# The first eight units of a two-block transformer kernel: the first unit split chunk by chunk, six units laid out in 8 KB runs, rotation tables loaded apart, and banks of their own for units 2 and 3 (counted from 0)

## What is computed

```python
normed = rms_norm(h, mix_norm_pre[0])
proj = normed @ w_in                       # 1024 x 6144
q, k, v, g = jnp.split(proj, [h * dk, 2 * h * dk, 2 * h * dk + h * dv], axis=-1)
q = rotate_pairs(q, cos, sin)
k = rotate_pairs(k, cos, sin) * (dk ** -0.5)
...                                        # decayed scores, o = scores @ v, norm, silu(g) * o, @ w_out
...                                        # FFN; block with sparse attention; FFN
...                                        # second block: gMLP and window attention, then 16 experts
```

## Time and profile before

| | us |
|---|---|
| median of 3 runs (2026.28 to 2027.13) | 2027.04 |
| the profiled execution's own time | 2029.09 |
| its span (first to last instruction) | 2027.3 |
| PE busy in the span | 1610.7 |
| DVE busy | 753.9 |
| ACT busy | 559.8 |

### The profile page before, as it was taken

How to read it: one execution, slowest core, us unless ns; L and a number is a source line. 1 busy time by engine, 2 the same in 40 slices (tenths; PEclk the granted TensorE clock), 3 DMA queues, 4 the chain that set the end, 5 groups by cost and what they waited for, 6 DMA issues and landing times.

```text
span 2027.3 us, 26324 instructions
## 1 busy us (share of the span) xinstructions
PE 1610.7 (79%) x11401; PEld 1109.1 (55%) x11401; DVE 753.9 (37%) x1094; ACT 559.8 (28%) x882; POOL 118.5 (6%) x105
## 2 busy tenths in 40 slices
PE   7999999999889999999998756566555555665655
PEld 7899999998569999897897211111111111111111
DVE  6766766675338755677655100000000000000000
ACT  4454544345545344445654000000000000000001
POOL 1001000000210200002300000000000000000000
PEclk9999999999889999999999887877888888778877
DMA  9844598657165555363267999999999999999996
GB/s 354 307 153 169 131 291 284 219 162 244 61 212 183 186 184 187 104 188 104 97 266 278 423 429 428 427 428 428 427 427 428 429 427 428 428 428 427 428 428 291
DMA packets 155161, 604.29 MB, mean 298 GB/s; under 512 B 6670, under 2 KB 107207, under 8 KB 127255
## 3 DMA queue, kind: packets, MB, share of 16 engines
q1 hardware_dynamic: 146224, 587.23, 73.5%
q10 hardware_dynamic: 7704, 11.24, 1.9%
q0 software_dynamic: 1136, 4.40, 1.7%
HBM read 595.51 MB, written 4.20 MB: 296 GB/s over the span
## 4 chain that ended last, share of the span: by engine, by line
PE 55%; DMA 34%; DVE 4%; another core or an unknown queue 3%; ACT 2%; issue 1%; POOL 0%; DVEq 0%; ACTq 0%
PE ps L768 19%; PE ps L837 12%; DMA arena<-in_w_exp_gate 7%; DMA late_expert_slots<-in_w_exp_gate 5%; DMA dense_ring<-in_w_exp_gate 5%; DMA late_expert_slots<-in_w_exp_up 5%; PE ps L1447 5%; DMA dense_ring<-in_w_exp_up 5%; PE ps L822 3%; DMA dense_tables<-in_w_exp_down 2%; DMA dense_ring<-in_w_exp_down 2%; DMA arena<-in_w_exp_down 2%; PE ps L1268 2%; PE ps L790 2%; PE ps L1476 1%
## 5 line engine op out<-in xcount | busy, mean ns | idle before, releaser
L650 DVE TENSOR_TENSOR split_operands<-dense_ring,split_operands 128x1024 fp32r<-128x1024 f32 x282 | 343.0, 1258 | 198.9 <-ACT split_operands L642 198.6
L768 PE MATMUL ps<-split_operands 128*128 128x256 f32 x3360 | 412.2, 284 | 3.1 <-DVE split_operands L650 1.9
L768 PEld LDWEIGHTS ps<-split_operands 128*128 128x128 f32 x3360 | 406.4, 192 | 6.2 <-issue 3.3
L642 ACT ACTIVATE split_operands<-dense_ring 128x1024 fp32r<-128x1024 f32 x284 | 284.5, 1050 | 305.7 <-PE ps L768 152.8
L2637 DVE TENSOR_TENSOR arena<-arena,ps 128x512 f32<-128x512 f32 x16 | 11.0, 688 | 563.0 <-PE ps L1447 563.0
L1938 ACT ACTIVATE arena<-ps 128x512 f32<-128x512 f32 x16 | 9.6, 597 | 585.3 <-PE ps L1447 585.3
L837 PE MATMUL ps<-split_operands 128*128 128x256 f32 x1248 | 154.0, 286 | 2.7 <-DVE split_operands L680 2.7
L837 PEld LDWEIGHTS ps<-split_operands 128*128 128x128 f32 x1248 | 152.6, 194 | 4.2 <-DVE split_operands L680 3.5
L837 PE MATMUL ps<-hidden_split,split_operands 128*128 128x256 f32 x960 | 118.6, 283 | 0.8 <-DVE split_operands L650 0.8
L837 PEld LDWEIGHTS ps<-hidden_split,split_operands 128*128 128x128 f32 x960 | 116.6, 192 | 1.0 <-DVE split_operands L650 1.0
L2645 DVE TENSOR_TENSOR tabs<-ps,tabs 128x512 f32<-128x512 f32 x16 | 11.1, 692 | 279.7 <-PE ps L1476 279.7
(11 more groups left out here) (371 smaller groups left out, 1780.8 us busy)
## 6 DMA issues: line engine op xcount, KB each, us to landing
dense_ring<-in_ffn_w_in SPq DMA_DIRECT2D x44, 1024.0 KB, 5.2
late_expert_slots<-in_w_exp_up SPq DMA_DIRECT2D x22, 2048.0 KB, 49.9
dense_ring<-in_w_exp_gate SPq DMA_DIRECT2D x21, 2048.0 KB, 50.7
arena<-in_w_exp_gate SPq DMA_DIRECT2D x20, 2048.0 KB, 49.6
arena<-in_w_exp_down SPq DMA_DIRECT2D x20, 2048.0 KB, 50.3
dense_ring<-in_w_exp_up SPq DMA_DIRECT2D x17, 2048.0 KB, 49.5
late_expert_slots<-in_w_exp_down SPq DMA_DIRECT2D x16, 2048.0 KB, 50.1
arena<-in_w_exp_up SPq DMA_DIRECT2D x14, 2048.0 KB, 50.2
```

The lines of the kernel that those rows point to most:

```text
L642: act.activation(w_hi[:, n % 2, c], ring[U % RING][:, c], ACT.Copy).then_inc(hi_ready, 1)
L650: dve.tensor_tensor(w_lo[:, n % 2, c], ring[U % RING][:, c], w_hi[:, n % 2, c], ALU.subtract).then_inc(lo_ready, 1)
L768: mm = pe.matmul(ps[:, bank, b * T:b * T + T], left, right, start=k == 0 and i == 0, stop=k == 7 and i == 2)
```

## The change

For the start: the small columns are issued by SP in front of everything instead of by ACT. The first six units come from a copy of the weights that the host has laid out so that each partition's 2048 floats are one run of 8 KB (before: eight runs of 1 KB). The first unit is split on ACT and DVE in eight chunks, each followed by the same chunk of the tokens, instead of in halves. The identity and rotation tables (896 columns) are loaded by SP between units 2 and 3; the other tables by ACT later, and `post` of the retention waits for them. The silu of the condition moves behind the squares on ACT. PE starts with 14 matmuls of `ones` into bank 6 (`warm`). The sums of squares (`norm`) move behind unit 1 on PE. For the rotation: units 2 and 3 write banks 2 and 3, units 4 to 7 write banks 5 and 7; PE waits for `qk_rot` before units 4 to 7 only. All splits up to unit 10 move one place forward on ACT and DVE, so the rotation of unit u now stands behind the low split of unit u + 3.

```diff
-for _name, _n in [("ident", 128), ("perm", 128), ("tri", 128), ("slot", 32), ("fold", 18), ("ret_cos", T), ("ret_sin", T),
+for _name, _n in [("perm", 128), ("tri", 128), ("slot", 32), ("fold", 18), ("ident", 128), ("ret_cos", T), ("ret_sin", T),
...
-FIRST_IN, BTAB_IN, REST_IN = 2 * 16, 2 * 16, 3 * 16
+FIRST_IN, BTAB_IN, REST_IN = 16, 5 * 16, 3 * 16
+FIRST_UNITS = 6
+QK_BANK = (5, 7, 2, 3, 5, 7, 5, 7)
... SP
-            first = col_src(w_in, 256 * order[0])
+            first = a["first_units"][0].rearrange("p (k n) -> p k n", k=8)
+            sp.dma_start(cols[:], a["cols"]).then_inc(cols_in, 16)
...
             for u in range(1, 24):
-                if 8 <= u < 16:
+                if u == 3:
+                    c = slice(TABS["ident"][0], TABS["rope_cos"][0])
+                    sp.dma_start(tabs[:, c], a["tabs"][:, c]).then_inc(first_in, 16)
+                if u < FIRST_UNITS:
+                    load(U_RET + u, a["first_units"][u], 0)
+                elif 8 <= u < 16:
... PE
+            def warm(n, bank, c0):
+                for _ in range(n):
+                    pe.matmul(ps[:, bank, c0:c0 + P], ones[:], ones[:], start=True, stop=True)
...
+            warm(14, 6, 0)
             for k in range(8):
-                if k % 4 == 0:
-                    pe.wait_ge(lo_ready, k // 4 + 1)
                 pe.wait_ge(xlo_ready, k + 1)
...
+            col_products(U_RET + 1, 7, lambda b, w, x: (w[:, b::2], x))
             norm(N_PRE0)
-            col_products(U_RET + 1, 7, lambda b, w, x: (w[:, b::2], x))
...
             for u in range(2, 8):
-                pe.wait_ge(qk_rot, u - 1)
-
-                col_products(U_RET + u, 5 + 2 * (u % 2), lambda b, w, x: (w[:, b::2], x))
+                if u >= 4:
+                    pe.wait_ge(qk_rot, u - 3 if u < 6 else u - 1)
+                col_products(U_RET + u, QK_BANK[u], lambda b, w, x: (w[:, b::2], x))
... ACT
+            for k in range(8):
+                if k % 4 == 0:
+                    act.wait_ge(x_in[k // 4], 16)
+                    act.wait_ge((half_landed, landed[0])[k // 4], 16)
+                ins = act.activation(w_hi[:, 0, k * T:k * T + T], ring[0][:, k * T:k * T + T], ACT.Copy)
+                if k % 4 == 3:
+                    ins.then_inc(hi_ready, 1)
+                act.activation(x_hi[:, k, :], h[:, k, :], ACT.Copy, scale=col("mix_pre0", k)).then_inc(xhi_ready, 1)
+            split_hi(act, U_RET + 1)
+            squares(N_PRE0, of_h)
             for r, name in enumerate(("c", "c_ctx")):
                 ins = act.activation(cs[:, :, r], col(name), ACT.Silu)
...
+            split_hi(act, U_RET + 2)
+            for dst, src in rests:
+                act.dma_start(dst, src).then_inc(btab_in, 16)
             roots(N_PRE0)
...
-            for u in range(2, 10):
+            for u in range(3, 10):
                 split_hi(act, U_RET + u)
... DVE
+            for k in range(8):
+                dve.wait_ge(x_in[k // 4], 16)
+                dve.wait_ge(xhi_ready, k + 1)
+                c = slice(k * T, k * T + T)
+                ins = dve.tensor_tensor(w_lo[:, 0, c], ring[0][:, c], w_hi[:, 0, c], ALU.subtract)
+                if k % 4 == 3:
+                    ins.then_inc(lo_ready, 1)
+                gained_lo(X_RET, "mix_pre0", k)
+            split_lo(dve, U_RET + 1)
             add_squares(N_PRE0)
-            split_lo(dve, U_RET + 1)
+            split_lo(dve, U_RET + 2)
             inverse(N_PRE0)
...
             for u in range(8):
-                split_lo(dve, U_RET + u + 2)
+                split_lo(dve, U_RET + u + 3)
                 taken(dve, U_RET + u)
                 if u >= 2:
                     dve.wait_ge(qk_done, u - 1)
-                src = ps[:, 5 + 2 * (u % 2), :]
+                src = ps[:, QK_BANK[u], :]
...
-                if u + 2 in ADA_RET_STEPS:
-                    ada_step(ADA_RET_STEPS.index(u + 2))
-            for u in range(10, 18):
+                if u + 3 in ADA_RET_STEPS:
+                    ada_step(ADA_RET_STEPS.index(u + 3))
+            for u in range(11, 18):
...
+            dve.wait_ge(btab_in, BTAB_IN)
             post(N_POST0, "mix_post0", U_F0, X_F0, "ffn_pre0")
```

More of the change, by code:

```diff
@@ L1491, in _ @@
         def _(act):
-            act.dma_start(cols[:], a["cols"]).then_inc(cols_in, 16)
-            firsts = [(tabs[:], a["tabs"]), (rel[0:32, :], a["rel_bias"])]
-            assert len(firsts) * 16 == FIRST_IN
+            first_tabs, late_tabs = TABS["ident"][0], TABS["rope_cos"][0]
+            rests = [(tabs[:, c], a["tabs"][:, c]) for c in (slice(0, first_tabs), slice(late_tabs, N_TABS))] + \
+                [(rel[0:32, :], a["rel_bias"])]
             def squares(n, src, ready=None):
@@ L1525, in _ @@
             ins.then_inc(constants_set, 1)
[L1526 to L1535, removed]
-            split_hi(act, U_RET + 1)
+            split_hi(act, U_RET + 2)
+            for dst, src in rests:
+                act.dma_start(dst, src).then_inc(btab_in, 16)
             roots(N_PRE0)
@@ L2035, in _ @@
             dve.wait_ge(cols_in, 16)
-            for half in range(2):
-                dve.wait_ge(x_in[half], 16)
-                for k in range(4 * half, 4 * half + 4):
-                    gained_lo(X_RET, "mix_pre0", k)
-                c = slice(half * UNIT // 2, (half + 1) * UNIT // 2)
-                dve.wait_ge(hi_ready, half + 1)
-                dve.tensor_tensor(w_lo[:, 0, c], ring[0][:, c], w_hi[:, 0, c], ALU.subtract).then_inc(lo_ready, 1)
+            for k in range(8):
[7 more added lines that the diff above has]
+            split_lo(dve, U_RET + 1)
             add_squares(N_PRE0)
-            split_lo(dve, U_RET + 1)
+            split_lo(dve, U_RET + 2)
             inverse(N_PRE0)
@@ L2071, in _ @@
             dve.wait_ge(first_in, FIRST_IN)
-            dve.wait_ge(first_in, FIRST_IN)
             o = TABS["ret_cos"][0]
@@ L2794, in pairs @@
         return pe.reshape(CMP_LEN // 2, 2 * HD).T
+    order = [c for hd in range(4) for c in (hd, 4 + hd)]
+    first_units = np.stack([in_rows(x["ret_w_in"][0][:, 256 * c:256 * c + 256]) for c in order[:FIRST_UNITS]])
     small = {"mix_pre0": x["mix_norm_pre"][0], "mix_pre1": x["mix_norm_pre"][1], "mix_post0": x["mix_norm_post"][0],
@@ L2815 @@
         "late_weights": np.concatenate([in_rows(x["cmp_w2_v"]), in_rows(x["w_router_2"][0])], axis=1),
-        "ret_w_in": x["ret_w_in"][0], "ret_w_out": x["ret_w_out"][0],
+        "first_units": first_units, "ret_w_in": x["ret_w_in"][0], "ret_w_out": x["ret_w_out"][0],
         "ffn_w_in0": x["ffn_w_in"][0], "ffn_w_in1": x["ffn_w_in"][1],
```

## The result

| | before | changed |
|---|---|---|
| median, us | 2026.66 (4 runs, 2025.39 to 2027.13) | 2038.63 (4 runs, 2036.17 to 2040.05) |
| profiled execution: own time, us | 2029.09 | 2038.67 |
| its span, us | 2027.3 | 2036.9 |

The changed kernel takes 1.0061 of the time before, with a 95% interval of 1.0048 to 1.0074: some 12 us slower.

The account below looks back on a forecast made before the run. It took PE's start of the v units (60.55 us) as the bound, later shifts reaching the end. Waits of 9.86 plus clock 4.6 minus front gain 2.9 gave +11.6 us, 2038.6 us for the median, range 2033.2 to 2042.

Parts of the forecast that it names:

- rotation step: PE before units 6 and 7: waits bare for rotations 4 and 5, 4.93 us each, a loss of 9.86 us.
- clock step: PE after the two pauses: the clock falls to 0.50, costing 2.3 us each, 4.6 us in all.
- Rival 1: PE's clock holds through both pauses before units 6 and 7: only +7.0 us, 2034.0 us; chance 0.12.
- front step: Start of the kernel up to unit 3: unit 3 starts at 28.8 us, a gain of 2.9 us (2.0 to 3.7).
- Rival 3: In the experts, later: loads found more landed make the loss good, end within 0.2%; chance 0.05.
- Rival 4: Front gives more and rounds are shorter, or one pause costs clock: 2035 to 2037 us; within main case, 0.80.
- Rival 2: Before units 6 and 7: rotation waits are covered, only the front gain stays, 2024.1 us; chance 0.03.

Follow-up runs that it names:

- e1: Changed kernel with DVE's rotation of unit u again behind the low split of unit u + 2; 0.9988 of the time before, median 2021.74 us.
- e2: Changed kernel with 22 fp32 matmuls of ones ahead of each rotation wait of units 6 and 7; 1.0057 of the time before, 2035.89 us.
- e4: e1 plus a one-element copy on ACT ahead of its waits, so the table load runs early; 0.9985 of the time before, 2022.16 us.
- e5: e4 with 26 instead of 14 warming matmuls, to keep PE busy until the first product; 0.9994 of the time before, 2024.74 us.
- e6: e5 with unit 3's low split on DVE ahead of the rotation of unit 0; 0.9990 of the time before, 2022.08 us.
- e8: Changed kernel measured again without any edit; 1.0067 of the time before, median 2038.30 us.
- e7: e6 without any warming matmuls of ones; 0.9990 of the time before, median 2024.70 us.
- e3: e1 without the 14 warming matmuls at the start; 1.0004 of the time before, median 2026.53 us.

## Why the prediction was right, and where it was not

**The rotation step held.** It forecast 4.93 us of bare waiting before each of units 6 and 7 and measured 4.86. e1 shows that the place of the rotations in DVE's order is the cause: undoing it takes the whole loss away. No third wait came before the v units, as forecast.

**The clock step held.** It forecast 2.3 us for each pause and measured 1.77 and 2.37, 4.14 together against 4.6. e2 shows that 3.7 of them belong to the idle PE. Rival 1, the clock that holds, would have left 5.76 us for both units. The advice of the Trainium skill in TensorE: Matmul & The Clock Gate (Part 1), to leave the ramp out of a model as under 1% of a span, would have missed about 4 us here. The measured 4.14 us are 0.2% of the span and so agree with its bound, but they are a third of what the change cost.

**The front step failed.** The prediction put unit 3 at 28.8 us, a gain of 2.9; it came at 31.69, a gain of 0.05, outside my bounds of 2.0 to 3.7. Behind unit 0 the step held: 12.60 us from there to unit 3, where I had 12.7. The miss lies in the start and in unit 0, and two statements about them were wrong.

The first is "The silu ... and its table load no longer stand ahead". The silu's load moved, but a load of 1.28 us still stands ahead of ACT's first instruction. Before the change the first load had cost nothing, because it ran long ahead of its silu, which waited for the columns until 5.64 us. The load for the root ran ahead as well, at 15.03 us, while its instruction waited for PE until 18.60. Both rows are from the kernel before:

```profile
1.38 1.28 ACT L1524 ACT_TABLE_LOAD   x1 [1.38 <-DVE cond_silu L1967]
...
18.60 0.38 ACT L1506 ACTIVATE root<-ps 128x256 f32<-128x256 f32 x1 [2.29 <-PE ps L744]
```

In the changed kernel the load ran behind the landing (7.25 us), bare on the path. Why it ran behind the wait there, and ahead of the wait in these two places, no run isolates. I had put the first product at 8.8 us and it came at 10.46: the load takes 1.30 of that (7.34 to 8.64), and ACT's release at 7.34 instead of 7.0 takes 0.34.

The other is the bound of 17.2 us for the end of unit 0; it ended at 19.09. I had allowed for part of unit 0 at the lower clock, but counted from a start at 8.8 us, and PE idled 3.58 us instead of the 1.7 that I had taken as a least value. Unit 0 then took 8.63 us, where my 16.1 us had left it 7.3. The ACT pairs were cheaper than my 0.8 us (8.64 to 9.36 is 0.72), which helped nothing while PE was the slower one. e4 repairs the load and e5 the pause; with both, and unit 3's low split ahead of the rotation (e6), the v units come 2.60 us earlier than before.

**How the total came out.** At the v units the sum was forecast as +11.6 us and measured as +13.79, so they start at 74.34 us, outside the 67 to 72 that I had written. The median moved by 11.97 us and the profiled span by 9.6. The span's smaller step is in part the one execution of before: its own time is 2.4 us above its median. The rest can be placed in the trace, but not explained by the change. The first matmul of L1268 (L1280 in the changed kernel) stands at 923.2 us before and at 935.0 in the changed kernel, so the shift is 11.8 there; in e8 it goes from 13.37 at the v units to 11.1, and in e1 from 0.53 to -2.5. That looks like a gain of 2 to 3 us on the way, but the same stretch, from the first v unit to that matmul, takes 862.7 us before, 860.7 in the changed kernel, 855.9 in e4 and 867.6 in e7, where the code differs by little more than a wait for the late tables. The granted clock of the stretch is 0.99 in e4 and 0.97 in e7 and before. So most of the spread of the time arises there: these executions of e4 and e7 took 2019.28 and 2029.05 us, though their v units start within 1 us of each other. Medians against medians, 12.0 and 12.6 us stand beside 13.8 and 13.4 at the v units; the rest of 1 to 2 us is within the spread. Rival 3, that much of the loss is made good later, is refuted for the greater part. The closeness of 2038.6 to 2038.63 is thus partly luck: the front came out 2.9 us worse than forecast, and the end 1.8 us better than the v units. Rival 4, a front that gives more, did not come: it gave less.

**Rival 2** (waits covered, faster) named the right point: with the waits gone the loss is gone (e1, 0.9988, interval up to 0.9999; its v units start 0.53 us later than before, so the front gain was not there yet). It did not need a third buffer of split weights, as I had written, only the old place of the rotation.

## What to carry to other kernels

When a prologue step is moved ahead in an in-order loop, look at what else the loop's body carries: here each split moved up one place, and the rotation behind it inherited a wait for a unit that PE had not yet run. List for each wait of the busiest engine which instruction releases it and what stands ahead of that on its own engine; a round that comes back to the waiting engine is bare time, and 4.86 us of idle PE cost some 2 us more in clock. Warming matmuls are worth what they bridge: end them where the first real product begins, and look in the trace where the table load runs; if it stands behind a transfer, a small copy that waits for nothing brings it ahead. Read a shift of a few us where it arises, for a later stretch of the same code can differ by more from one execution to the next (855.9 to 867.6 us here).

## What the runs showed of the hardware that was not expected

- ACT's table load can run ahead of the wait of the instruction behind it or after it. It ran at 1.38 us with its silu at 5.64, and at 15.03 us with its root at 18.60, in the kernel before; but at 7.34 us, behind a transfer that landed at 7.25, in the changed kernel. With a copy ahead that waits for no transfer it ran at 0.77 us. What decides is open.
- After 5.8 us of warming matmuls, which reached the full pace only from 6.1 us on, and a pause of 3.58 us, unit 0 ran its first 28 or so matmuls at the lower level of 1.2 GHz and took 8.63 us. Other executions with 14 warming matmuls and a pause had 7.52 (e2) to 8.29 us (e8), those with none 7.56 (e3) and 7.98 (e7), so this warming gave nothing that shows. With PE busy to the first product unit 0 took 6.34 us (e6).
- The executions of one kernel spread over up to 10 us in the later measurements (before: 2021.0 to 2031.2), where the first three stood within 0.9 us. With that spread a shift of 2.6 us at the start is at the edge of what some twelve executions resolve.
